# The recurrent layer's features in tiles of 128, first jobs by depth, and two stages of each second layer merged

## What is computed

```python
def mlstm_mixer(x, w_in, conv_w, conv_b, w_qkv, gate_b, norm_g, skip, mem_k, mem_v):
    h = x @ w_in                                   # 1024 -> 768 + 768 + 16 + 256
    xm, z, gates, q_mem = jnp.split(h, [ML_W, 2 * ML_W, 2 * ML_W + 4 * ML_HEADS], axis=-1)
    xc = conv over 5 neighbouring tokens of xm, per feature
    xc = jax.nn.silu(xc + conv_b)
    q, k, v = per head (4 heads of 192): xc @ w_qkv[0], xc @ w_qkv[1], xm @ w_qkv[2]
    g = gates + gate_b
    hs = recurrence forward + recurrence backward  # chunks of 128 tokens
    hs = normed per head, * norm_g
    y = (hs + skip * xc) * jax.nn.silu(z)
    return jnp.concatenate([y, memory_attention(q_mem, mem_k, mem_v)], axis=-1)
```

## Time and profile before

| | us |
|---|---|
| time, median of 3 runs | 3996.92 (3995.92 to 4001.78) |
| the profiled execution's time | 3996.58 |
| its span, first to last instruction | 3994.9 |
| TensorE busy in the span | 3496.1 (88%) |
| VectorE busy | 1966.6 (49%) |
| ScalarE busy | 1405.2 (35%) |
| mean granted TensorE clock | 0.917 of full |

### The profile page before, as it was taken

How to read it: one execution, slowest core, us unless ns; L and a number is a source line. 1 busy time by engine, 2 the same in 40 slices (tenths; PEclk the granted TensorE clock), 3 DMA queues, 4 the chain that set the end, 5 groups by cost and what they waited for, 6 DMA issues and landing times. The chain is left out here.

```text
span 3994.9 us, 52000 instructions
## 1 busy us (share of the span) xinstructions
PE 3496.1 (88%) x20111; PEld 2741.3 (69%) x20111; DVE 1966.6 (49%) x3420; ACT 1405.2 (35%) x2595; POOL 361.4 (9%) x289
## 2 busy tenths in 40 slices
PE   7999996999869988848969999599889789998878
PEld 6874474888738766646658888389755577885547
DVE  4526554758444535464445746523255433325554
ACT  2016631657440023233135645500254320124441
POOL 0100000333210000000013233100000000000000
PEclk9999997999978988878979999799789898987999
DMA  6425024779553110013147867401000211100011
GB/s 208 157 78 176 22 80 146 277 282 396 217 199 111 62 30 1 1 32 95 64 150 281 338 236 284 190 32 40 15 1 1 95 55 47 42 23 1 1 67 71
DMA packets 250172, 459.91 MB, mean 115 GB/s; under 512 B 44835, under 2 KB 119927, under 8 KB 249593
## 3 DMA queue, kind: packets, MB, share of 16 engines
q1 hardware_dynamic: 231513, 389.70, 28.1%
q0 software_dynamic: 18432, 67.12, 4.4%
HBM read 380.72 MB, written 73.33 MB: 114 GB/s over the span
## 5 line engine op out<-in xcount | busy, mean ns | idle before, releaser
L1710 PE MATMUL psum<-high_in,e_rowsT_high 128*128 128x256 f32 (+1 forms) x1080 | 330.1, 324 | 5.4 <-DVE e_rowsT_low L174 5.4
L1711 PE MATMUL psum<-high_in,e_rowsT_low 128*128 128x256 f32 (+1 forms) x1080 | 326.1, 320 | 0.0
L174 POOL TENSOR_TENSOR low_down<-w_down,high_out 128x1024 fp32r<-128x1024 f32 x64 | 196.5, 3087 | 321.1 <-ACT high_out L1784 321.1
L1710 PEld LDWEIGHTS psum<-high_in,e_rowsT_high 128*128 128x128 f32 x1080 | 206.4, 191 | 22.3 <-issue 6.1
L1711 PEld LDWEIGHTS psum<-high_in,e_rowsT_low 128*128 128x128 f32 x1080 | 206.9, 192 | 16.2
L251 PE MATMUL psum<-ring_high,s_x_high 128*128 128x512 f32 (+3 forms) x768 | 139.9, 326 | 28.9 <-DVE ring_high L169 28.9
L3366 DVE TENSOR_REDUCE mla_low<-psum 128x1 f32<-128x256 f32 (+7 forms) x128 | 91.0, 753 | 147.7 <-PE psum L3232 147.7
L1839 POOL COPY e_index<-moe_ids 128x1 uint32 (+1 forms) x49 | 9.6, 195 | 1548.0 <-POOLq L84 922.5
L174 DVE TENSOR_TENSOR low_gate<-w_gate,high_in 128x1024 fp32r<-128x1024 f32 x128 | 148.0, 1219 | 0.6 <-issue 0.6
L174 DVE TENSOR_TENSOR low_up<-w_up,high_in 128x1024 fp32r<-128x1024 f32 x128 | 148.0, 1219 | 0.0
L251 PEld LDWEIGHTS psum<-ring_high,s_x_high 128*128 128x128 f32 x768 | 117.2, 196 | 40.8 <-DVE ring_high L169 29.3
(11 more groups left out here) (594 smaller groups left out, 8155.7 us busy)
## 6 DMA issues: line engine op xcount, KB each, us to landing
w_gate<-in_exp_w_gate SPq DMA_DIRECT2D x32, 2048.0 KB, 10.1
w_up<-in_exp_w_up SPq DMA_DIRECT2D x32, 2048.0 KB, 15.1
w_down<-in_exp_w_down SPq DMA_DIRECT2D x32, 2048.0 KB, 21.8
ada<-in_ada_w SPq DMA_DIRECT2D x24, 1024.0 KB, 7.1
expert_rows<-e_out POOLq DMA_DIRECT2D x47, 512.0 KB, 7.0
expert_rows<-zero_row SPq DMA_DIRECT2D x33, 512.0 KB, 7.0
token_rows<-x SPq DMA_DIRECT2D x32, 512.0 KB, 2.6
x<-token_rows SPq DMA_DIRECT2D x24, 512.0 KB, 7.0
```

What stands on the lines that cost most here:

```text
L174: return eng.tensor_tensor(low, whole, high, ALU.subtract)
L1710: pe.matmul(dst, rows_high[:, k, :], w_high[:, k, cols], start=(k == 0), stop=False)
L1711: pe.matmul(dst, rows_low[:, k, :], w_high[:, k, cols], start=False, stop=False)
```

## The change

- *Recurrent layer's projection.* Features in tiles of 128 (6 tiles of xm, 6 of z). The 16 gate columns become the stationary side of 2 feature jobs with 512 moving tokens; the gates come out turned and are turned back by 8 transposes in `gates_and_values`. 8 chunks and 30 jobs, in the order xm, z, gates and queries. The first chunk's weights are loaded in the stage before (`gathered_norm`, `following`), behind its loads of x. The first chunk's 4 jobs run together, depth tile by depth tile (`first_chunk`), VectorE splitting weights and rows per depth tile. ScalarE takes x's highs ahead of the activation of `c_col`. The taps are loaded behind chunk 1. `Modulation` gets a pace (3 chunks per weight chunk) and a list of due jobs for this layer; `Conv` does its six tiles at jobs 18 to 26 in steps of one, two, one, one, one. Only this projection is by depth: the others get x split already. `BiasTable.load` of the first layer does nothing, so its move changes nothing.
- *What follows.* A head's 192 features are now pieces of 128 and 64 rows of two tiles (`pieces_of`) in the values' and the per-head products; `head_norm` and the residual product have 6 and 8 tiles of depth, and `shared_high` is off.
- *Second layers.* `modulated_rows` goes into `project` (`ModulatedFront`): x is turned half by half of the tokens, ScalarE modulates 128 x 512 at a time, VectorE splits by halves, and the first weight chunk's DMA is issued at the stage's start. `transpose_rows` goes into `gated_residual`: w_out is loaded in five pieces for the first 512 columns and one for the rest, behind x and the gate; the first half's 8 token tiles are computed together by depth (`OutPlan.ORDER`), the second half tile by tile.

```diff
@@ project
+    by_depth = split_x
@@ sync
-            if beside:
-                beside.load(sp, s)
             for c, (view, _) in enumerate(chunks):
-                if c < ahead:
+                if c == 0 and prefetched:
+                    sp.wait_ge(prefetched, 16)
+                    sp.sem_inc(loaded[0], 16)
+                elif c < ahead:
                     sp.sem_inc(loaded[c % 2], 16)
...
+                if beside and c == 1:
+                    beside.load(sp, s)
@@ tensor
+            if front:
+                front.turn(pe, s)
+            def first_chunk():
...
+                for k in range(KT):
+                    pe.wait_ge(s["first_high"], k + 1)
+                    pe.wait_ge(s["x_high"], k + 1)
+                    for n in range(int(ends[0])):
+                        pe.matmul(dst[n], *parts[n][0][k], start=(k == 0), stop=False)
+                    pe.wait_ge(s["first_low"], k + 1)
+                    pe.wait_ge(s["x_low"], k + 1)
+                    for n in range(int(ends[0])):
+                        pe.matmul(dst[n], *parts[n][1][k], start=False, stop=False)
+                        mm = pe.matmul(dst[n], *parts[n][2][k], start=False, stop=(k == KT - 1))
...
@@ vector
+            if front:
+                front.make_diagonal(dve, s)
+                front.split(dve, s, 0)
+            if by_depth:
+                raw, high, low = slot(0), slot(0, highs), slot(0, lows)
+                dve.wait_ge(loaded[0], 16)
+                for k in range(KT):
+                    take_high(dve, high[:, k, :], raw[:, k, :]).then_inc(s["first_high"], 1)
+                    dve.wait_ge(s["first_high"], k + 1)
+                    leave_low(dve, low[:, k, :], raw[:, k, :], high[:, k, :]).then_inc(s["first_low"], 1)
                     dve.wait_ge(s["x_high"], k + 1)
-                    leave_low(dve, low, whole, high).then_inc(s["x_low"], 1)
+                    leave_low(dve, x.low[k], x.whole[k], x.high[k]).then_inc(s["x_low"], 1)
+                split_weights(1)
+            else:
+                split_weights(0)
+            if front:
+                front.split(dve, s, 1)
@@ gathered_norm, sync
+            if following:
+                dst, view, fetched = following
+                sp.dma_start(dst, view).then_inc(fetched, 16)
@@ ml_layer
-    chunks = [(w[:, :, c * 192:(c + 1) * 192], feature_jobs(0, 2, HF, into(c))) for c in range(4)]
-    chunks.append((w[:, :, 1536:1680], token_jobs(0, 16, lambda e, ps, t: copy_out(e, gates[:, t, :], ps)) + feature_jobs(16, 1, P, keep_qm(0))))
...
+    jobs = [feature_jobs(0, 2, P, into(c)) for c in range(3)] + [feature_jobs(0, 2, P, keep_z(c)) for c in range(3)]
+    jobs += [feature_jobs(0, 1, 16, keep_gates) + feature_jobs(16, 1, P, keep_qm(0)), feature_jobs(0, 1, P, keep_qm(1))]
...
-    weights = OutWeights(loads, raws, lows, highs, True)
+    weights = OutWeights(loads, raws, lows, highs, False)
@@ ModulatedFront
+    def turn(self, pe, s):
+        for n in range(2 * KT):
+            half, k = divmod(n, KT)
+            if k == 0:
+                pe.wait_ge(s["diag_ready"], 4 * half + 4)
+            if half:
+                pe.wait_ge(s["x_whole"], k + 1)
...
+    def ready(self, pe, s, n):
...
+        if n < BANKS:
+            pe.wait_ge(s["x_whole"], KT + n + 1)
+        if n in (0, 4):
+            pe.wait_ge(s["x_high"], KT * (1 + n // 4))
+            pe.wait_ge(s["x_low"], KT * (1 + n // 4))
...
+    def split(self, dve, s, half):
+        dve.wait_ge(s["rows_turned"], KT * (half + 1))
...
@@ gated_residual
+    ORDER = (2, 3, 4, 5, 0, 1, 6, 7)
+    PIECES = ((2, 3), (3, 4), (4, 6), (0, 2), (6, 8))
...
+            for n, (lo, hi) in enumerate(plan.PIECES):
+                sp.dma_start(w_out[0][:, lo:hi, :], weights[:, lo:hi, 0:BANK]).then_inc(loaded[n], 16)
             sp.dma_start(x[:, :, :], rows).then_inc(s["x_loaded"], 16)
             sp.dma_start(gate[:, :], broadcast_rows(gate_row)).then_inc(s["gate_loaded"], 16)
+            sp.dma_start(w_out[1][:, :, :], weights[:, :, BANK:D]).then_inc(loaded[-1], 16)
...
+            highs, lows = (mix_high, latent_high), (mix_low, latent_low)
+            for i, k in enumerate(plan.ORDER):
+                last = i == KT - 1
+                pe.wait_ge(s["w_high"], i + 1)
...
@@ build_program
-    core.modulations = [Modulation(core, l, AT_WORK + at * KB) for l, at in enumerate((80, 64))]
+    core.modulations = [Modulation(core, 0, AT_WORK + 80 * KB, AT_WORK + 116 * KB, 2, [(c,) for c in range(Modulation.CHUNKS)]),
+                        Modulation(core, 1, AT_WORK + 64 * KB, AT_WORK + 116 * KB, 3, [(0,), (1, 2), (3,), (4, 5), (6,), (7, 8), (9,), (10, 11)])]
```

More of the change, by code:

```diff
@@ L185, in tiles_of, with project @@
     return [tile[:, k, :] for k in range(tile.shape[1])]
-def project(nc, core, chunks, slots, x, lows=None, highs=None, beside=None, ahead=0, modulation=None):
+def project(nc, core, chunks, slots, x, lows=None, highs=None, beside=None, front=None, ahead=0, modulation=None, prefetched=None):
     jobs = [(c, job) for c, (_, js) in enumerate(chunks) for job in js]
@@ L232, in _ @@
         def _(pe):
+            if front:
+                front.turn(pe, s)
+            def first_chunk():
+                dst = [core.bank[n][0:jobs[n][1][1][0], 0:jobs[n][1][1][1]] for n in range(int(ends[0]))]
+                parts = [[jobs[n][1][0](slot(0, w), part) for w, part in ((highs, x.high), (lows, x.high), (highs, x.low))] for n in range(int(ends[0]))]
+                for k in range(KT):
[8 more added lines that the diff above has]
+                        mm = pe.matmul(dst[n], *parts[n][2][k], start=False, stop=(k == KT - 1))
+                        if k == KT - 1:
+                            mm.then_inc(s["products_ready"], 1)
+            if by_depth:
+                first_chunk()
             for n, (c, (pairs, shape, _)) in enumerate(jobs):
+                if by_depth and c == 0:
+                    continue
+                if front:
+                    front.ready(pe, s, n)
                 dst = core.bank[n % banks][0:shape[0], 0:shape[1]]
@@ L3440, in second_layer @@
     early = EarlyMixers(core, l, r_qk, r_vz[:, :, RET_W:], gate[:, :, :], g2[:, :, GATE_RANK:])
-    project(nc, core, chunks, slots, x_parts, lows, highs, beside=early)
+    project(nc, core, chunks, slots, front.x, lows, highs, beside=early, front=front)
     x = m.at("s_x", AT_X, [P, TILES, D])
@@ new lines, in gated_residual, with of_rows @@
+    weights = rows_of(w_dram)
+    def of_rows(in_mix, in_latent, k):
+        return in_latent[:, k - 2, :] if k in plan.LATENT else in_mix[:, k if k < 2 else k - 4, :]
+    with stage(nc, *[f"weights_loaded{n}" for n in range(len(plan.PIECES) + 1)], "x_loaded", "gate_loaded", "gain_loaded", "turned", "mix_high", "mix_low",
+               "latent_high", "latent_low", "w_high", "w_low", "products_ready", "gated", "added", "stored", "squared", "root_ready", "rms_ready",
+               "scaled") as (block, s):
+        loaded = [s[f"weights_loaded{n}"] for n in range(len(plan.PIECES) + 1)]
@@ L3514, in _ @@
+            pe.wait_ge(s["w_high"], 2 * KT)
+            pe.wait_ge(s["w_low"], 2 * KT)
+            for t in range(TILES):
+                pe.wait_ge(s["gated"], t + 1)
                 for k in range(KT):
-                    if n == 0:
-                        pe.wait_ge(s["high_ready"], 2 * k + 2)
-                    pe.matmul(core.bank[n % BANKS], mix.high[k][:, rows_], w_high[:, k, cols], start=(k == 0), stop=False)
+                    product(1, t, k, highs, w_high, first=(k == 0))
                 for k in range(KT):
-                    if n == 0:
-                        pe.wait_ge(s["low_ready"], 2 * k + 2)
@@ L3521, in _ @@
-                    pe.matmul(core.bank[n % BANKS], mix.high[k][:, rows_], w_low[:, k, cols], start=False, stop=False)
-                    mm = pe.matmul(core.bank[n % BANKS], mix.low[k][:, rows_], w_high[:, k, cols], start=False, stop=(k == KT - 1))
+                    product(1, t, k, highs, w_low)
+                    mm = product(1, t, k, lows, w_high, last=(k == KT - 1))
                 mm.then_inc(s["products_ready"], 1)
```

461 lines of the change are left out of this document (251 added, 210 removed).

## The result

The changed kernel takes **3928.44 us** (median of 3, 3923.25 to 3931.67) against 3996.92 before: the ratio is 0.9824, with a 95% interval from 0.9802 to 0.9846. It is 68 us faster, where 218 were forecast, and lies far above the range of 3757 to 3818. The profiled execution has a span of 3926.8 us and a mean granted clock of 0.903, lower than the 0.917 before, although the work is shorter.

A forecast was written before the change was run, and what follows sets the result against it. The prediction took TensorE, busy 88% of a 3994.9 us span, as the bound. Its terms -102.7 - 7 - 30.8 - 36 - 42 = -218.5 took 3996.6 to 3778 us, range 3757 to 3818.

The forecast's parts named there:

- B: Recurrent layer's gates, values and per-head products: no change, 0 us, with bounds of 0 to +38.
- rival 4: Values and per-head products: 192 changes of row form drain TensorE, +19 us at 0.1 each (3797), 3817 at 0.2; chance 9%.
- Rival 3: Clock not given back at once after short gaps or starved starts, and in gate jobs: +20 us, 3798; chance 14%.
- A: Recurrent layer's projection: 176 us against 278.7, a gain of -102.7 us.
- rival 2: Recurrent projection: VectorE sets the pace and TensorE waits at later chunks, 12 to 35 us, 3790 to 3813; chance 12%.
- C: Head normalization: six feature tiles instead of eight and shorter silus, -7 us, bounds -5 to -11.
- E: Recurrent layer's residual product: K = 10 becomes K = 8, -30.8 us, bounds -24 to -31.
- F: Fronts of the two second layers: -18 us each, -36 together, bounds -28 to -40.
- G: Gated residuals of the second layers: -21 us each, -42 together, bounds -32 to -44.

The follow-up runs named there:

- 64 + 64 rows: The kernel before, but both pieces of a head take only rows 0 to 63 of their 96 in values and products: 4130.40 us, one run.
- full rows: The changed kernel, but every piece of a head in values and per-head products has 128 rows, the neighbouring head's rows meeting zero weights: 3775.7 us.

## Why the prediction was wrong

**B, the step that failed.** The prediction put values and products at 0, with 0 to +38 as bounds, "by the row" of the memory attention. Three things were wrong with that.
- The row. The earlier trace rows shows one change from four 64-row instructions to eight 128-row ones, and the prediction reads in it the absence of a gap between modelled ends. But the pause is there, in the starts. Asked for a narrow stretch, the same view splits the x4 row:

```profile
1811.50 0.64 PE L821 MATMUL psum<-mem_kT,ml_qm 64*128 64x256 f32 x2
```

From the pair before (1811.07) to this one it is 0.43 us, and from this one to the first 128-row instruction (1812.07) 0.57: 0.14 us more stood at the change. Times 192 that is 27 us, inside the bounds and not the zero that was taken. The runs give 0.24 and 0.29 us at the lower clock and 0.18 at the upper one, so the upper bound of 0.2 was too low as well. By the stretches that makes (3.8 + 4.6) x 4 in the products, 12.5 in the values' last 104 instructions and 2.8 in their first 24: 49 us. That part of rival 4 was right in kind and too small.
- The clock. No term of B had it. Rival 3 put it at the starts and the gate jobs, where it didn't happen: the gate jobs took 5.55 us at 1.00. It happened in work in which the busy row shows TensorE full. Its name for it, the clock that isn't given back at once, fits what was seen: the lower level from a head's start on, never left in the products. By the runs with 64 + 64 rows (no pauses, lower level) and with full rows (no pauses, upper level) the clock alone costs 37.8 - 21.8 = 16 us per head and about 17 us in the values' last 104 instructions, 34.2 against 17.3, with 2 in the first ones: 64 + 17 + 2 = 83 us. In the products 128 + 64 rows with half of the pauses did not lose it.
- What follows. The recurrence of each head starts at the lower level and needs to come back: from the end of the products to the next head's it takes 52.9 us (1547.32 to 1600.19) against 46.6 (1389.15 to 1435.79) with full rows, 6.3 per head, 25 us.

49 + 83 + 25 = 157, against 157.6 measured between the changed kernel and the one with full rows.

The Trainium skill's rule ("TensorEngine Tiling (Array Packing)", Key Properties: "Changing tiling mode (not just tile) drains the TensorE") agrees with the pauses: 0.18 to 0.29 us at each step over 64 rows, none between 96 and 72. The page says nothing at that place of the granted clock, which took 83 us, and 108 with what follows, against 49 for the pauses. The rule stood in the prediction with 9%, against one pair of rows that, read by its starts, speaks for it.

**A** was right: -102.3 for -102.7 between the prediction's own ends. The first chunk took 24 us for the 25 forecast; the gap before TensorE's first product was 4.25 us; TensorE waited for nothing after it, so the cover of zero on VectorE held, and rival 2 did not come. The wait for modulation columns is gone.

**C** was -13.9 for -7. The six tiles gave 5.2 and the silus 1.9, as forecast. The rest is z's transfer, which I had left at its old length and whose gain was only a bound (-11): ScalarE waited 17.10 us for it before and 10.19 after, 3 MB into 128 partitions instead of 96. The other profiles agree: 10.0 to 10.6 us wherever z has tiles of 128, 16.7 to 17.1 wherever it has tiles of 96.

```profile
1762.70 7.68 ACT L2408 ACTIVATE hn_z<-hn_z 96x1024 f32<-96x1024 f32 x8 [17.10 <-DMA hn_z<-gate_rows]
```

```profile
1810.02 5.79 ACT L2445 ACTIVATE hn_z<-hn_z 128x1024 f32<-128x1024 f32 x6 [10.19 <-DMA hn_z<-gate_rows]
```

Taken at its end the sum would have been 3774.

**E, F, G** were right: -30.6 for -30.8, -35.8 for -36, -39.9 for -42. Each G came 1 us later than worked out.

**The rest.** The first layer's memory attention, which the change doesn't touch, took 5.4 us more. Its clock was 0.50 from 495 to 505 us in this execution. It was 1.00 there in before and in seven other profiles, 0.90 and 0.89 in two, and 0.55 in one, of a kernel whose instructions up to there are those of before. So it differs between executions of the same work, and is no part of the change.

The best test of the sum is the kernel with full rows: all parts of the change but the short pieces, 3775.7 us where 3778 was forecast. That the two are so close is in part luck: C gives 7 us more than its term, and the stage before the projection took 5 us more in its profile than before (89.2 against 84.0), which no term had.

## What to carry to other kernels

When a change cuts a contraction into uneven pieces, count the steps over 64 rows and the rows at work, and look at the granted clock of the stretch, not only at whether TensorE is busy: 128 + 64 rows in turn cost a pause and the upper clock, while the same work with the missing rows filled with zeros cost nothing that the stretch shows (309.4 us against 311.7 before). If padding is impossible, give neighbouring jobs the same form at their seam; it needs no more instructions, though here it brought the clock back in the products and not in the values. And a row that shows no gap bounds a cost only down to the spread of that row: write it as a bound, not as zero, and look at the single starts on both sides of the seam.

## What the runs showed of the hardware

- TensorE's granted clock was 0.50 through whole stretches in which it was busy without a gap. Past the first microseconds of a head, the products of 96 + 96 and 128 + 128 rows stood at the upper level; 64 + 64, 72 + 72, 96 + 72 and 96 + 64 at the lower one; 128 + 64 at the lower one with a change of form at every piece, and at the upper one with half or a quarter of the changes. The values of 128 + 64 rows stayed at the lower one with half of the changes too.
- Rows that meet zero weights count as rows here: the pieces filled up to 128 rows ran at 1.00.
- A step from more than 64 rows to 64 or back took 0.24 us (512 columns) to 0.29 us (192 columns) at the lower clock, about 0.18 at the upper one. In the kernel before, in the memory attention, it took 0.14 more at the seam of 64 and 128 rows. A step from 96 to 72 rows took nothing.
- 16 stationary columns with 512 moving ones cost 5.55 us a job of 24 matmuls, at clock 1.00, and the next jobs, with 128 stationary columns from the same weight chunk, 5.60 (5.44 elsewhere); 16 moving columns stood at 0.57.
- 3 MB from DRAM were there after 10.0 to 10.6 us of waiting into 128 partitions, and after 16.7 to 17.1 into 96, in all twelve profiles.
